# A hybrid decoder step on one core: phase tables moved forward through memory, and expert outputs added onto the residual rows by indirect writes

## What is computed

```
wts = wts / sum(wts)                         # two experts per row
act = silu(t @ w_gate[e]) * (t @ w_up[e]) * combine[t, e]
x = x + gt2 * sum_e act @ w_down[e]          # gt2: one row for the prompt, one per decode row
y = rms_norm(x, final_g)
```

## Time and profile before

| | |
|---|---|
| time, median of 3 runs | 1297.97 us (1297.96 to 1301.45) |
| the profiled execution | 1301.65 us, span 1300.0 us |
| mean granted TensorE clock | 0.929 of full speed |
| PE busy | 1118.5 us, 86% of the span |
| DVE busy | 548.8 us, 42% |
| ACT busy | 306.0 us, 24% |
| POOL busy | 231.9 us, 18% |
| moved by DMA | 173.49 MB, mean 133 GB/s |

### The profile page before, as it was taken

How to read it: one execution, slowest core, us unless ns; L and a number is a source line. 1 busy time by engine, 2 the same in 40 slices (tenths; PEclk the granted TensorE clock), 3 DMA queues, 4 the chain that set the end, 5 groups by cost and what they waited for, 6 DMA issues and landing times. The chain is left out here.

```text
span 1300.0 us, 15152 instructions
## 1 busy us (share of the span) xinstructions
PE 1118.5 (86%) x5094; PEld 675.3 (52%) x5095; DVE 548.8 (42%) x1234; ACT 306.0 (24%) x684; POOL 231.9 (18%) x364
## 2 busy tenths in 40 slices
PE   4899998999976997667869799996499999889876
PEld 4466665447756776465654445543244444444332
DVE  4153344414365356888942433545411111111128
ACT  5121112342125233122214323232011111101033
POOL 0100000003323241544440000102311111101050
PEclk8999999999989989688879899997699999999887
DMA  9557091000132002434417100006378565798373
GB/s 349 167 205 259 6 290 65 1 1 9 30 68 65 2 2 74 136 133 139 139 23 294 66 17 33 32 33 149 105 259 257 166 219 170 246 323 289 110 276 131
DMA packets 124704, 173.49 MB, mean 133 GB/s; under 512 B 36430, under 2 KB 80195, under 8 KB 124639
## 3 DMA queue, kind: packets, MB, share of 16 engines
q1 hardware_dynamic: 113644, 138.51, 32.7%
q0 software_dynamic: 7376, 21.59, 5.0%
q10 hardware_dynamic: 3626, 12.64, 2.4%
HBM read 127.40 MB, written 44.24 MB: 132 GB/s over the span
## 5 line engine op out<-in xcount | busy, mean ns | idle before, releaser
L2066 PE MATMUL bank<-w_out,H 128*128 x384 | 171.9, 601 | 10.0 <-DMA w_out<-in_w_up 5.2
L350 PE MATMUL bank<-hT,w_ring 128*128 128x344 f32 x576 | 169.5, 456 | 3.8 <-ACT hT L533 3.8
L350 PEld LDWEIGHTS bank<-hT,w_ring 128*128 128x128 f32 x576 | 110.0, 192 | 62.2 <-issue 5.2
L2066 PEld LDWEIGHTS bank<-w_out,H 128*128 128x128 f32 x384 | 72.3, 192 | 107.0 <-issue 107.0
L2346 PE MATMUL bank<-w_out,hT 128*128 128x512 f32 (+1 forms) x288 | 127.5, 595 | 0.5 <-DVE hT L1858 0.5
L435 PE MATMUL bank<-w_ring,hT 128*128 128x512 f32 x256 | 114.7, 605 | 3.6 <-DVE ZO L766 3.6
L2130 DVE TENSOR_TENSOR H<-H,bank 128x256 f32<-128x256 f32 x24 | 10.1, 421 | 245.4 <-ACT H L2101 245.4
L2050 PE MATMUL bank<-y1T,H 128*128 x192 | 91.3, 619 | 10.7 <-DVE H L2139 7.9
L435 PEld LDWEIGHTS bank<-w_ring,hT 128*128 128x128 f32 x256 | 64.2, 254 | 49.5 <-issue 32.1
L2346 PEld LDWEIGHTS bank<-w_out,hT 128*128 128x128 f32 (+1 forms) x288 | 50.1, 179 | 64.5 <-issue 63.7
L2050 PEld LDWEIGHTS bank<-y1T,H 128*128 128x128 f32 x192 | 35.4, 194 | 52.3 <-issue 52.3
(11 more groups left out here) (518 smaller groups left out, 1836.2 us busy)
## 6 DMA issues: line engine op xcount, KB each, us to landing
ys_d<-ZO SPq DMA_DIRECT2D x18, 1024.0 KB, 13.4
y1T<-in_w_down SPq DMA_DIRECT2D x16, 1024.0 KB, 5.6
w_out<-in_w_gate SPq DMA_DIRECT2D x16, 1024.0 KB
w_out<-in_w_up SPq DMA_DIRECT2D x16, 1024.0 KB
ys_d<-H ACTq DMA_DIRECT2D x24, 512.0 KB, 5.6
w_ring<-in_w_in SPq DMA_DIRECT2D x4, 2048.0 KB, 8.7
y1T<-in_w_ada SPq DMA_DIRECT2D x4, 2048.0 KB, 8.2
hT<-in_w_ada SPq DMA_DIRECT2D x4, 2048.0 KB, 13.1
```

Of the source, the lines that this page charges most:

```text
L350: mm = t.matmul(ps[3 * (m % 2) + s][:, 0:SEG], w_ring[:, q % 2, k, (m % 4) * P:(m % 4 + 1) * P], hT[:, k, s * SEG:(s + 1) * SEG], start=(k ...
L2066: mm = t.matmul(ps[2 + p][:, :], xT[p][:, k, :], wgu[:, bass.ds(buf, 1), k, :].rearrange("p o n -> p (o n)"), start=(k == 0), stop=(k == K ...
```

## The change

Three things change together.

The phase tables of all four parts are built in the input block, DVE and POOL together, right after DVE's L831, and SP writes each finished table (512 KB) to `e_d`; the third and fourth part reuse the room of the first and second once those are written. ACT at `b == 8` waits until all eight are written, since one table lies in `crow_room`. The S5 block only loads them. To make `ph` ready, DVE's work on the S5 constants is moved between the convolution tiles: rates after tile 5, first power after 8, inputs after 9, powers 2 to 5 after 10, powers 6 to 8 after 11 (ahead of the `gate_rows` copy). SP loads the constants earlier. PE's small transposes move to after tile 4.

The zeroing of `ys_d` (18 DMAs of 1 MB) goes, since `ys_d` goes. The residual rows `X2` are written to `acc_d` as they are made, and the gate rows to `gate_d`. The lists hold pairs: row number and weight, where unused places name 128 distinct rows past the end. The weights are worked out in `choose`.

In the expert block POOL, for each slot, copies the pair (`keep`), gathers the matching gate rows from `gate_d`, and adds the weighted and gated result onto `acc_d` by an indirect write with addition (`put`), whose landing it waits for. The multiplication by weight and gate is DVE's (`out`), straight from PSUM; ACT's two copies and its write go. At the end SP loads `acc_d` tile by tile, and ACT, DVE and SP only norm and write.

```diff
@@ input block, SyncE
+                for q in range(4):
+                    dve.wait(sp, f"e{q}_7")
+                    sp.dma_start(e_d[q, 0], Es_(q, 0)).then_inc(e_out[q % 2], 16)
+                    pool.wait(sp, f"e{q}_7")
+                    sp.dma_start(e_d[q, 1], Es_(q, 1)).then_inc(e_out[q % 2], 16)
@@ input block, ScalarE, b == 8
                         pe.wait(a, "pick7")
+                        a.wait_ge(e_out[0], 64)
+                        a.wait_ge(e_out[1], 64)
                         for x in range(3):
                             act.did(a.activation(sqT[:, x * SEG:(x + 1) * SEG], ps[5 + x][:, 0:SEG], ACT.Copy), "ss_rows")
@@ input block, VectorE (after each convolution tile m)
+                    if m == 5:
+                        rates()
+                    elif m == 8:
+                        first_power()
+                    elif m == 9:
+                        inputs()
+                    elif m == 10:
+                        powers(2, 6)
+                    elif m == 11:
+                        powers(6, LAGS + 1)
+                pe.wait(v, "gate_rows")
...
+                power_copies()
+                eighth_angle()
                 v.wait_ge(hp_land, 32)
                 act.wait(v, "gates")
                 dve.did(v.tensor_tensor(sp_t[:, 0], gates[:, :, 4:8], bc(hp[:, 0, :], [P, 9, HEADS], 1), ALU.add), "absx")
...
+                tables(0)
+                tables(1)
+                tables(2)
+                tables(3)
                 act.wait(v, "ln")
@@ S5 block
+                for c in range(2):
+                    load_phases(sp, c)
                 for c in range(2):
                     load_ada(sp, c)
...
+                    if q in (1, 2):
+                        dve.wait(sp, f"zc{q - 1}")
+                        pool.wait(sp, f"zl{q - 1}")
+                        load_phases(sp, q + 1)
...
-                phases(0)
...
-                    if q < 3:
-                        phases(q + 1)
...
-                    pool.wait(v, f"e{q}_7")
+                    v.wait_ge(e_land[q % 2], 32 * (q // 2 + 1))
@@ router, VectorE, at the end of choose(r)
+                    for j, oh in enumerate((one, two)):
+                        tt(m_, oh, lg[:, lo:hi, :], ALU.mult)
+                        dve.drain(v)
+                        dve.did(v.tensor_reduce(col[:, 2 + j, lo:hi], m_, AX.X, ALU.add))
+                    tt(col[:, 4, lo:hi], col[:, 2, lo:hi], col[:, 3, lo:hi], ALU.add)
+                    dve.drain(v)
+                    dve.did(v.reciprocal(col[:, 4, lo:hi], col[:, 4, lo:hi]))
+                    dve.drain(v)
+                    for j in range(2):
+                        dve.did(v.tensor_tensor(pairs_f[:, 2 * lo + j:2 * hi:2, 1], col[:, 2 + j, lo:hi], col[:, 4, lo:hi], ALU.mult))
@@ expert block, GpSimd
+            def gather(n, p):
+                g.wait_ge(who_in[p], n * 16 + 16)
...
                 g.indirect_dma_start(xin[p][:, :], None, h2_d, bass.IndirectOffsetOnAxis(ap=who[p][:, 0:1], axis=0)).then_inc(x_in[p], 16)
+            def keep(n, p, s):
+                g.wait_ge(x_in[p], n * 16 + 16)
...
+                g.tensor_scalar(which_i[p], who[p][:, 0:1], float(1 - SEQ), 0.0, ALU.add, ALU.max).then_inc(which, 1)
+                g.tensor_copy(kept_i[p], who[p]).then_inc(kept, 1)
+                g.wait_ge(kept, s + 1)
+                g.wait_ge(which, s + 1)
...
+                g.indirect_dma_start(gate_rows_[p], None, gate_d, bass.IndirectOffsetOnAxis(ap=which_i[p], axis=0)).then_inc(gate_in[p], 16)
+            def put(n, p, s):
+                g.wait_ge(y_half, s + 1)
+                g.wait_ge(y_sb, s + 1)
...
+                g.indirect_dma_start(acc_d, bass.IndirectOffsetOnAxis(ap=kept_i[p][:, 0:1], axis=0), yo[p][:, :], None,
+                                     compute_op=ALU.add).then_inc(y_out[p], 16)
+                g.wait_ge(y_out[p], n * 16 + 16)
+                g.sem_inc(y_free[p], 1)
             def body(it):
+                for p in range(2):
+                    s = it * 2 + p
+                    if not isinstance(it, int):
+                        put(it - 1, p, s - 2)
+                    keep(it, p, s)
+                    list_in(s + 2, p)
+                    g.wait_ge(xT_ps, s + 1)
+                    gather(it + 1, p)
+            def tail(it, s):
+                put(it, 0, s - 1)
+                put(it, 1, s)
+                g.sem_inc(y_done, 1)
@@ expert block, VectorE, after x_copy of the body
+            def out(it, p, s):
+                v.wait_ge(dn_ps, s + 1)
+                if not (isinstance(it, int) and it == 0):
+                    v.wait_ge(y_free[p], it + 1)
+                v.wait_ge(kept, s + 1)
+                v.wait_ge(gate_in[p], it * 16 + 16)
+                for half_, done in ((0, y_half), (1, y_sb)):
+                    c = slice(half_ * 512, (half_ + 1) * 512)
+                    v.scalar_tensor_tensor(out=yo[p][:, c], in0=ps[5 + half_][:, :], scalar=kept_f[p][:, 1:2], in1=gate_rows_[p][:, c],
+                                           op0=ALU.mult, op1=ALU.mult).then_inc(done, 1)
@@ end, SyncE; fin_gpsimd and fin_tensor are deleted
+            sp.wait_ge(y_done, 1)
+            for i in range(9):
+                n = P if i < NT else DEC
+                sp.dma_start(ya[i][0:n, :], acc_d[i * P:i * P + n, :]).then_inc(ygot[i], 16)
```

More of the change, by code:

```diff
@@ L750, in _ @@
                 dve.drain(v)
[L751 to L766, removed]
                 w = lambda n: w4[:, n]
@@ L785, in _ @@
[L785 to L794, removed]
@@ new lines, in tables @@
+                def tables(q):
+                    gs, Ec, Es = slice(q * NG, (q + 1) * NG), phase(q, 0), phase(q, 1)
+                    if q >= 2:
+                        v.wait_ge(e_out[q % 2], 32)
+                    dve.did(v.memset(Ec[:, :, 0:1], 1.0))
+                    dve.did(v.tensor_copy(Ec[:, :, 1:2], ph[:, 0, gs].unsqueeze(2)), f"e{q}_0")
+                    wd = 1
+                    while wd < NCH:
+                        step = wd.bit_length()
+                        pool.wait(v, f"e{q}_{step - 1}")
+                        cw, sw = (x[:, :, wd:wd + 1].to_broadcast([P, NG, wd]) for x in (Ec, Es))
+                        tt(e1[:, :, 0:wd], Ec[:, :, 1:wd + 1], cw, ALU.mult)
+                        tt(e2[:, :, 0:wd], Es[:, :, 1:wd + 1], sw, ALU.mult, wait=False)
+                        tt(Ec[:, :, wd + 1:2 * wd + 1], e1[:, :, 0:wd], e2[:, :, 0:wd], ALU.subtract, f"e{q}_{step}")
+                        wd *= 2
@@ L2014, in moe_gpsimd @@
             g.wait_ge(h2_out, 16 * 9)
-            load(0, 0)
+            g.wait_ge(x1_out, 16 * 9)
+            g.wait_ge(zland, 48)
+            gather(0, 0)
             dve.wait(g, "slots")
             list_in(1, 1)
-            pairs(g, body)
+            gather(0, 1)
+            pairs(g, body, tail)
         def moe_tensor(t):
@@ L2101, in body @@
                     a.activation(sg[p][:, :], ps[2 + p][:, 0:FE], ACT.Silu).then_inc(silu_sb, 1)
-                    if not (static and s == 0):
-                        out(it - 1 + p, 1 - p, s - 1)
-            def tail(it, s):
-                out(it, 1, s)
-                for p in range(2):
-                    a.wait_ge(y_out[p], it * 16 + 16)
-                    a.activation(sg[p][:, 0:1], sg[p][:, 0:1], ACT.Copy).then_inc(silu_sb if p == 0 else y_done, 1)
             dve.wait(a, "slots")
-            pairs(a, body, tail)
+            pairs(a, body)
         def moe_vector(v):
@@ L2404, in _ @@
                     scores(i)
+                pe.wait(a, "gt2")
+                dve.wait(a, "H2_8")
+                for half_ in range(2):
+                    c = slice(half_ * 512, (half_ + 1) * 512)
+                    act.did(a.activation(gt2P[:, c], ps[2 + half_][:, :], ACT.Copy))
+                    act.did(a.activation(gt2D[:, c], ps[(7, 4)[half_]][0:DEC, :], ACT.Copy), "gt2")
                 moe_scalar(a)
```

458 lines of the change are left out of this document (216 added, 242 removed).

## The result

The changed kernel takes 1365.6 us (median of 4 runs, 1362.68 to 1371.95), against 1298.49 for the kernel before (median of 4): a ratio of 1.051 (1.048 to 1.054). The forecast was 1306, the range 1262 to 1350. The sign was right and the size was not. The profiled run took 1362.68 with a span of 1361.1. All ratios and their 95% intervals use fast runs alone, which leaves out one run of lists_ahead (1328.13 us, clock 0.91).

A forecast was written before the change was run, and what follows sets the result against it. PE was taken to bound the expert block, DVE the S5 block, nothing the end; POOL would then set slots. 1289.8 + 33 - 14.5 gave a 1308.3 span against 1300.0, so 1306 us on the median; range 1262 to 1350.

The forecast's parts named there:

- Input block, +17: Input block: added powers and four phase tables make ACT's copies for `ss_rows` start 17 us later (14 to 21).
- S5 block, -32: S5 block: with the tables removed, its four parts together save 32 us (25 to 35).
- Router: Router: eight small DVE operations added to each `choose`, partly hidden beside PE, cost 1.7 us.
- Expert block: Expert block: POOL's serial line sets the slot at 14.5 us instead of PE's 12.4.
- X + 8.0: Expert block: length of POOL's line per slot, X for the adding write plus 8.0 us for all other steps.
- X: Expert block: issue and landing of POOL's adding write, taken as 6.5 us (3.3 to 10); 24 us of time per us.
- slow-write rival: Expert block: adding write takes 8.5 us as DMA contention feeds on itself; slot 16.5, 1354 us; chance 0.19.
- rival of tables for nothing: Input and S5 blocks: tables cost 21 and give 25, first half worth 4 instead of 15; 1317; chance 0.08.
- End, 33: End: last write 33 us after the last addition (28 to 38), limited by writing out of two buffers.

The follow-up runs named there:

- lists_ahead: The changed kernel with each slot's list loaded two slots earlier and the gather taking its rows from a copy: 1315.23 us, ratio 1.0137.
- tables_only: The kernel before with only the phase tables moved to the input block, written to memory and loaded by the S5 block: 1297.95 us, ratio 0.9974.
- overlapped: The changed kernel with POOL's line re-ordered: lists two slots ahead, next gather before the adding write, landing awaited late: 1286.24 us, ratio 0.9891.
- plain_write: The changed kernel with the indirect write overwriting rows instead of adding, so the sum over experts and residual is left out: 1339.62 us, ratio 1.026.
- no_gate_gather: The changed kernel without the gate rows' gather, POOL's line in the old order, decode rows' own gates left out: 1338.30 us, ratio 1.027.
- small_weights: The changed kernel with weight loads of experts 2 to 15 cut to an eighth (gate, up) and a sixteenth (down): 1327.09 us, ratio 1.021.

## Why the prediction was wrong

**Input block, +17: right within its range.** In the changed kernel the last table holds up `ss_rows`: PE's `ss` product comes 14.6 us later, the last product of the ring 16.7, the delta block's end 17.4.

**S5 block, -32: right in kind, and not a constant.** Gained were 28.5 us from the first transposes to those behind the block (153.1 to 124.6), inside the 25 to 35; in tables_only, 21.7, outside them. Parts are 28.8 to 30.3 apart instead of the forecast 27.5, with DVE waiting for PE as said. I had let the clock cost a tenth of PE's part, 1.7 us; these two traces of nearly the same instructions differ by 6.8.

**Router:** up to its end the forecast holds to 2.6 us: the first row gather came 10.4 us earlier, forecast 13.

**Expert block: the step that failed, by size.** "X + 8.0" with X = 6.5, 14.5 a slot, was 16.9. By term: write and going on 8.12 instead of 6.8; the operations before the gate gather 1.19 instead of 0.8; the gate's issue 1.08 instead of 1.26; list load to gather 5.12 instead of 4.4; gather 1.42 instead of 1.27. More than half of the 2.4 us, 1.3, is X with its handing over. Of that, 0.6 is the typical value: the median from the write's issue to the next step was 7.4 (median landing 7.0). The other 0.75 is the mean above that median: a line in which each step waits for the last adds up means, and the mean was 8.1, with landings up to 10.1. The list load is the clearer case: its median, 4.5, is the 4.4 of the forecast, and its mean is 5.12. I had worked from the earlier trace rows by their medians, while their upper sides reach 3 us above them, and had taken 4.4 beside a row of 6.1 in the earlier trace rows. X alone would not have left the range: 1.3 us at 24 us each are 32, which gives 1338. The other terms add 1.1 us a slot, 24 us more, and carry the time beyond 1350. Twenty-two slots at 2.4 are 53 us; from the first write to the last landing it took 386.4 us instead of 335.1, 51.3 more. The first write was 4.7 us later than forecast (944.9 against 940.2) and the end 3.2 shorter, which gives the 1361.1 instead of 1308.3.

By the Trainium skill's rule (Collectives: The Full Stack, "The bandwidth ceiling: the fold count and why AG ≠ RS ≠ AR") that adding moves half as much, an undisturbed adding write would take 5.6, an estimate. The shortest was 5.9, and an added MB kept the DMA engines busy about twice as long as a plain one (last section): the trace agrees. The mean among other transfers, 8.1 to the next step, is not in that estimate.

**Mechanism and rivals.** The place was right: overlapped keeps the bytes, changes the order of POOL's line, adds one small copy a slot, and gives back 79 us. The slow-write rival (X = 8.5, 1354) was the nearest, and its reason only in part: contention with the weights holds 1.8 of the 4.5 us, and 2.7 are in the line with hardly a weight load beside it. Contention did not feed on itself: at overlapped's pace, with the DMA engines at 83%, the median landing was still 7.0. The rival of tables for nothing had its number in tables_only (3.4 us, its price was 4) and not beside overlapped (14 us). The clock followed: in the expert block it was 0.89, and the down products took 754 ns each (L2150 above); in overlapped, where PE waits less, it was 0.97 (930 to 1250 us) and they took 631.

**End, 33: 29.8.** The two output buffers limit it as forecast: two tiles take 3.96 us, 1.98 each, forecast 2.05:

```profile
1349.69 1.28 DVE L2286 SCALAR_TENSOR_TENSOR V<-w_out,small,V 128x1024 f32<-128x1024 f32 x1 [0.98 <-DMA out_y_p<-V]
1351.25 1.28 DVE L2286 SCALAR_TENSOR_TENSOR V<-w_out,small,V 128x1024 f32<-128x1024 f32 x1
1353.65 1.28 DVE L2286 SCALAR_TENSOR_TENSOR V<-w_out,small,V 128x1024 f32<-128x1024 f32 x1 [0.98 <-DMA out_y_p<-V]
```

## What to carry to other kernels

When one engine issues several transfers in a loop and waits for one of them, write its line down step by step and sum it with mean landings under load, not medians; if the sum is above the pace of the bounding engine, the order of the line can be worth more than any single step (here 79 us, against 50, 27 and 26 for the three steps that were changed by themselves). Issue what does not depend on the landing first (the next gather, the next list), and wait where the next conflicting write stands. The gain of an edit ahead of other stages can depend on what surrounds it, here 3 or 14 us for the same tables: judge it in more than one kernel.

## What the runs showed of the hardware

An indirect write that adds keeps POOL 1.62 us for its issue, a plain one 1.01. Software queue q0 (first row the changed kernel, then plain_write, both from 935 to 1270 us; packets, MB, share of 16 engines):

```profile
q0 software_dynamic: 8982, 30.52, 36.2%
```

```profile
q0 software_dynamic: 9443, 32.09, 27.4%
```

Per MB that is 4.0 and 2.9 us of all 16 engines. About a third of the first row's bytes are additions, so by an estimate from these two rows an added MB takes some 6 us, twice a plain one.

A small load in the software queue takes longer behind a large gather issued just before it. The 1 KB list lands in 3.6 us (median) behind the gate rows' 512 KB in the changed kernel and in 2.0 without them in no_gate_gather; to the gather that needs it, 4.5 and 2.8. With the weight loads cut it is still 4.2 (small_weights), so the weights are not the reason.

A GpSimd operation on the indices and the indirect DMA that reads them stand 1.0 us apart, 0.81 to 0.84 of it idle, in every slot (L2074 to L2079 in the changed kernel).
